# Four transformer layers on one NeuronCore: layer-norm sums taken from the additions and ScalarE, narrow products after the first wide one

## The reference, cut to what matters

```python
def layer_norm(x, g, b):
    mu = jnp.mean(xf, axis=-1, keepdims=True)
    var = jnp.mean(jnp.square(xf - mu), axis=-1, keepdims=True)
    return (xf - mu) * lax.rsqrt(var + LN_EPS) * g + b

# layers 0 and 1 (first_block)
mix = hybrid_mixer(x, w_in[l], ...)    # h @ w_in, split in nine parts: latent attention and
                                       # sparse top-64 attention, @ w_o
x = layer_norm(ALPHA * x + mix, ln1_g[l], ln1_b[l])
ffn = grouped_moe(x, ...)              # 16 experts, 2 for each token
x = layer_norm(ALPHA * x + ffn, ln2_g[l], ln2_b[l])

# layer 2: hgrn2_mixer (recurrent), layer 3: swa_sink_mixer (sliding window), each then
h = layer_norm_2(ALPHA_2 * h + mix, ln_mix_g[layer], ln_mix_b[layer])
ff = conv_ffn(h, ...)                  # 1024 -> 5632, convolution of width 3, gate, -> 1024
h = layer_norm_2(ALPHA_2 * h + ff, ln_ffn_g[layer], ln_ffn_b[layer])
# after layer 2, from its output: keys and values that layer 3 uses
k_flat, v_flat = jnp.split(h @ shared_w_kv, 2, axis=-1)
```

## Time and profile before

| | before |
|---|---|
| runs, us | 1381.19, 1379.75, 1381.02 (median 1381.02) |
| profiled execution, us | 1381.08 |
| its span, us | 1379.3 |
| mean granted TensorE clock (1 is full speed) | 0.981 |
| TensorE busy | 1309.4 us (95%) |
| weight loads on TensorE | 975.9 us (71%) |
| VectorE busy | 776.9 us (56%) |
| ScalarE busy | 563.9 us (41%) |
| GpSimd busy | 109.4 us (8%) |
| transfers | 347.64 MB, mean 252 GB/s |
| instructions | 20,721 |

### The profile page before, as it was taken

The page is one execution under the profiler, slowest core; times in us unless marked ns, Lnnn a source line. Parts: engine busy times, 40 slices in busy tenths (PEclk is TensorE's granted clock), DMA queues, the critical chain, the costliest instruction groups (busy, mean ns, idle before and its releaser), DMA issues.

```text
span 1379.3 us, 20721 instructions
## 1 busy us (share of the span) xinstructions
PE 1309.4 (95%) x8104; PEld 975.9 (71%) x8104; DVE 776.9 (56%) x1462; ACT 563.9 (41%) x1012; POOL 109.4 (8%) x130
## 2 busy tenths in 40 slices
PE   7989999999899999999989999999999988999997
PEld 7867444444686764344339988899998876999985
DVE  3976312112578651112145799877775676577766
ACT  4563211211446431111124335276654473466552
POOL 1030000000001200000002362000000011000000
PEclk9999999999999989999998999999999999999999
DMA  9338899999744579999997437685756520656630
GB/s 304 134 149 331 352 421 421 421 421 421 244 151 183 217 289 423 421 421 421 421 384 233 147 102 116 153 272 183 243 213 209 182 70 1 214 183 198 245 136 31
DMA packets 130072, 347.64 MB, mean 252 GB/s; under 512 B 10277, under 2 KB 86331, under 8 KB 105412
## 3 DMA queue, kind: packets, MB, share of 16 engines
q1 hardware_dynamic: 125232, 332.29, 63.9%
q0 software_dynamic: 3888, 13.55, 4.3%
q10 hardware_dynamic: 868, 0.63, 0.1%
HBM read 342.25 MB, written 4.19 MB: 251 GB/s over the span
## 4 chain that ended last, share of the span: by engine, by line
PE 70%; DVE 14%; DMA 7%; SPq 4%; ACT 2%; issue 2%; POOL 0%; DVEq 0%; ACTq 0%
PE bank L2032 12%; PE bank L1857 9%; PE bank L1858 8%; PE bank L1859 8%; PE bank L2043 6%; SPq L664 4%; DMA slot<-in_w_up 4%; PE bank L2366 3%; PE bank L2370 3%; PE bank L2368 3%; DMA slot<-in_ffn_w_in 2%; PE bank L1742 2%; PE bank L1808 2%; PE bank L1869 1%; DVE ln_stats L1190 1%
## 5 line engine op out<-in xcount | busy, mean ns | idle before, releaser
L1857 PE MATMUL bank<-x_high,w_high 128*128 128x256 f32 x1040 | 295.7, 284 | 0.0
L1858 PE MATMUL bank<-x_low,w_high 128*128 128x256 f32 x1040 | 294.4, 283 | 0.0
L1859 PE MATMUL bank<-x_high,w_low 128*128 128x256 f32 x1040 | 294.3, 283 | 0.0
L793 ACT ACTIVATE w_high<-slot 128x1024 fp32r<-128x1024 f32 x214 | 215.6, 1054 | 178.5 <-PE bank L1859 78.9
L2032 PE MATMUL bank<-slot,arena 128*64 128x512 f32 x976 | 223.0, 592 | 1.6 <-DMA slot<-in_w_up 1.6
L1857 PEld LDWEIGHTS bank<-x_high,w_high 128*128 128x128 f32 x1040 | 199.7, 192 | 1.8 <-issue 1.7
L1858 PEld LDWEIGHTS bank<-x_low,w_high 128*128 128x128 f32 x1040 | 199.8, 192 | 0.1
L1859 PEld LDWEIGHTS bank<-x_high,w_low 128*128 128x128 f32 x1040 | 199.7, 192 | 0.0
L2032 PEld LDWEIGHTS bank<-slot,arena 128*64 128x64 f32 x976 | 73.3, 137 | 142.5 <-issue 142.3
L1635 DVE TENSOR_TENSOR w_low<-slot,w_high 128x1024 fp32r<-128x1024 f32 x88 | 104.0, 1222 | 58.2 <-ACT w_high L793 58.2
L1456 DVE TENSOR_TENSOR arena<-arena,bank 128x512 f32<-128x512 f32 x16 | 11.0, 688 | 200.9 <-PE bank L2032 200.9
(11 more groups left out here) (345 smaller groups left out, 2196.9 us busy)
## 6 DMA issues: line engine op xcount, KB each, us to landing
slot<-in_w_gate SPq DMA_DIRECT2D x62, 1024.0 KB, 19.6
slot<-in_w_up SPq DMA_DIRECT2D x60, 1024.0 KB, 19.0
slot<-in_w_down SPq DMA_DIRECT2D x60, 1024.0 KB, 18.7
slot<-in_ffn_w_in SPq DMA_DIRECT2D x44, 1024.0 KB, 7.5
slot<-in_ffn_w_out SPq DMA_DIRECT2D x22, 1024.0 KB, 5.0
slot<-in_hgrn_w_in SPq DMA_DIRECT2D x16, 1024.0 KB, 6.7
slot<-in_w_in SPq DMA_DIRECT2D x10, 1024.0 KB, 9.8
slot<-in_w_o SPq DMA_DIRECT2D x8, 1024.0 KB, 4.9
```

Source lines behind the costliest of these rows:

```text
L793: return nc.scalar.activation(dst, src, ACT.Copy)
L1857: mm(dst, high[:, k, :], x_high[:, k, :], start=(k == 0), stop=False)
L1858: mm(dst, high[:, k, :], x_low[:, k, :], start=False, stop=False)
L1859: last = mm(dst, low[:, k, :], x_high[:, k, :], start=False, stop=(k == KD - 1))
```

## The change

**Norm.** The statistics and the aggregate go. The residual addition of each half also writes its row sum (`accum_out`) to `ln_sum`; after the experts it is the last addition of the pairs that does so. One 128x1 operation makes minus the mean from the two sums. ScalarE squares `res` with minus the mean as bias over 1024 columns and sums the squares (`accum_out`), and takes the root of that over 1024. VectorE centres with minus the mean into `x_tok` instead of `res`. In the norms behind the mixers and for the `z` norm, the order of ScalarE's roots and copies of tile 0 and 1 changes, and where `xT` is wanted in tile 1, it is copied after `x_high`.

**Waits.** The first wide product behind a norm waits for `x_high` by half: its steps 0 to 3 need only the first half of tile 1, its steps 4 to 7 the second. VectorE's `x_low` of tile 1 waits for the `xT` copies too.

**Order and banks.** `narrow(l, 1)` and `values(1)` come behind the first half of the first wide product, between its "hw" and its "x" pass. The narrow product gets a bank of its own, `ki`, where it shared `ikdk` with a wide one.

```diff
-        for n, by in (("f2", "ikdk"), ("f1", 1), ("c", 2), ("iq", 4), ("a", 6), ("b", 8), ("d", 10),
+        for n, by in (("f2", "ki"), ("f1", 1), ("c", 2), ("iq", 4), ("a", 6), ("b", 8), ("d", 10),
...
                 act.wait_ge(sem("ln_moments"), 2 * k + t + 1)
-                nc.scalar.activation(ln_std[:, t:t + 1], ln_mv[:, t, 1:2], ACT.Sqrt, bias=eps[:, 0:1]).then_inc(sem("ln_root"), 1)
+                link(nc.scalar.activation(arena[:, D * t:D * (t + 1)], res[:, t, :], ACT.Square, bias=ln_minus_mean[:, t:t + 1],
+                                          accum_out=ln_squares[:, t:t + 1]))
+                nc.scalar.activation(ln_std[:, t:t + 1], ln_squares[:, t:t + 1], ACT.Sqrt, bias=eps[:, 0:1], scale=1.0 / D).then_inc(sem("ln_root"), 1)
...
+                late = y == "z"
+                if k is not None:
+                    for t in range(1 if late else NT):
+                        std_of(k, t)
                 for t in range(NT):
-                    if k is not None and (t == 0 or not whole):
-                        std_of(k, t)
-                    if whole:
+                    if whole and t == 0:
                         copies(t, xT, "x_whole")
-                    if k is not None and whole and t == 0:
-                        std_of(k, 1)
+                        if late:
+                            std_of(k, 1)
                     copies(t, x_high, "x_high_ready")
+                    if whole and t:
+                        copies(t, xT, "x_whole")
...
+                b = produced(act, (l, "ki"))
+                drained(copy(A["ikdk"][0:N_KI, 0, :], b[0:N_KI, 0:T]), (l, "ki"))
                 b = produced(act, (l, "ikdk"))
-                copy(A["ikdk"][0:N_KI, 0, :], b[0:N_KI, 0:T])
-                drained(copy(A["ikdk"][:, 1, :], b[:, T:2 * T]), (l, "ikdk"))
+                drained(copy(A["ikdk"][:, 1, :], b[:, 0:T]), (l, "ikdk"))
...
-                            ins = V.scalar_tensor_tensor(res[:, t, cols], x_tok[:, t, cols], ALPHA, b[:, :], ALU.mult, ALU.add)
+                            ins = V.scalar_tensor_tensor(res[:, t, cols], x_tok[:, t, cols], ALPHA, b[:, :], ALU.mult, ALU.add, accum_out=ln_sum[:, t, h:h + 1])
                             drained(ins, (l, f"{y}{t}{h}"))
+                    if from_psum:
+                        for h in range(2):
                             evacuated(dve, (l, f"{y}{t}{h}"))
-                        last = V.bn_stats(ln_stats[:, t, h, :], res[:, t, cols])
-                    link(last)
-                    V.bn_aggr(ln_mv[:, t, :], ln_stats[:, t, :, :].rearrange("p a b -> p (a b)")).then_inc(sem("ln_moments"), 1)
+                    for n in (t,) if from_psum else range(NT if t == 0 else 0):
+                        V.tensor_scalar(ln_minus_mean[:, n:n + 1], ln_sum[:, n, 0:1], ln_sum[:, n, 1:2], -1.0 / D, ALU.add, ALU.mult)\
+                            .then_inc(sem("ln_moments"), 1)
                     dve.wait_ge(sem("ln_moments"), 2 * k + t + 1)
                     if k in (1, 3):
                         dve.wait_ge(sem("ln2_rows"), 32 * (k // 2 + 1))
                     else:
                         dve.wait_ge(sem("ln_rows"), 32 * ([0, 2, 4, 5, 6, 7].index(k) + 1))
-                    link(V.scalar_tensor_tensor(res[:, t, :], res[:, t, :], ln_mv[:, t, 0:1], ln_gb[:, 0, :], ALU.subtract, ALU.mult))
+                    link(V.scalar_tensor_tensor(x_tok[:, t, :], res[:, t, :], ln_minus_mean[:, t:t + 1], ln_gb[:, 0, :], ALU.add, ALU.mult))
                     dve.wait_ge(sem("ln_root"), 2 * k + t + 1)
                     link(V.reciprocal(ln_std[:, t:t + 1], ln_std[:, t:t + 1]))
                     for h, ready in enumerate(("ln_half", "ln_done")):
                         cols = slice(512 * h, 512 * (h + 1))
-                        V.scalar_tensor_tensor(x_tok[:, t, cols], res[:, t, cols], ln_std[:, t:t + 1], ln_gb[:, 1, cols], ALU.mult, ALU.add)\
+                        V.scalar_tensor_tensor(x_tok[:, t, cols], x_tok[:, t, cols], ln_std[:, t:t + 1], ln_gb[:, 1, cols], ALU.mult, ALU.add)\
                             .then_inc(sem(ready), 1)
...
+                    if t and whole_before is not None:
+                        dve.wait_ge(sem("x_whole"), 4 * whole_before + n + 1)
...
+                            if p < PAIRS - 1:
+                                drained(V.tensor_tensor(r, r, b[:, :], ALU.add), (l, f"M{t}{h}{p}"))
+                            else:
+                                drained(V.scalar_tensor_tensor(r, r, 1.0, b[:, :], ALU.mult, ALU.add, accum_out=ln_sum[:, t, h:h + 1]), (l, f"M{t}{h}{p}"))
...
-            def passes(dst, n, ab, kinds, t=None, first=False, last=False):
-
-                x = slice(0, T) if t is None else tok(t)
-                d = dst[:, T * ab:T * (ab + 1)] if t is None else dst[:, T * ab + P * t:T * ab + P * (t + 1)]
+            def passes(d, n, ab, kinds, first=False, last=False, new_x=None):
+
                 for k in range(KD):
+                    if new_x is not None and k % 4 == 0:
+                        pe.wait_ge(sem("x_high_ready"), new_x + 3 + k // 4)
                     for kind in kinds:
                         weight = (w_low if kind == "w" else w_high)[n % 2][:, ab, k, :]
-                        ins = mm(d, weight, (x_low if kind == "x" else x_high)[:, k, x], start=(first and k == 0 and kind == "h"),
+                        ins = mm(d, weight, (x_low if kind == "x" else x_high)[:, k, :], start=(first and k == 0 and kind == "h"),
...
+            def first_pair(name, n, new_x, tokens, i=None, between=None):
+
+                b = reuse(pe, name, i)
+                for ab in range(2):
+                    d = b[:, T * ab:T * (ab + 1)]
+                    pe.wait_ge(sem("split"), 2 * n + ab + 1)
+                    passes(d, n, ab, "hw", first=True, new_x=new_x)
+                    if ab == 0:
+                        if between is not None:
+                            between()
+                        transposes_out(*tokens)
+                    last = passes(d, n, ab, "x", last=True)
+                done(last, name)
...
+                return product(b[0:N_KI, tok(t)], lambda c: s2[:, c, :], lambda c: xT[:, c, tok(t)], KD)
...
-                b = narrow(l, 1)
+                b = reuse(pe, (l, "ikdk"))
                 pe.wait_ge(sem("split"), 2 * IN_UNIT[l] + 1)
-                pe.wait_ge(sem("x_high_ready"), 4 * (l + 1))
-                for k in range(KD):
-                    mm(b[:, T:2 * T], w_high[0][:, 0, k, :], x_high[:, k, :], start=(k == 0), stop=False)
-                    mm(b[:, T:2 * T], w_low[0][:, 0, k, :], x_high[:, k, :], start=False, stop=False)
+                passes(b[:, 0:T], IN_UNIT[l], 0, "hw", first=True, new_x=4 * l)
+                done(narrow(l, 1), (l, "ki"))
                 transposes_out(*((l - 1, "m") if l else (0, "in")))
-                for k in range(KD):
-                    last = mm(b[:, T:2 * T], w_high[0][:, 0, k, :], x_low[:, k, :], start=False, stop=(k == KD - 1))
-                done(last, (l, "ikdk"))
+                done(passes(b[:, 0:T], IN_UNIT[l], 0, "x", last=True), (l, "ikdk"))
...
-                b = reuse(pe, (l, "U00"), 0)
-                pe.wait_ge(sem("x_high_ready"), before_x + 4)
-                for ab in range(2):
-                    pe.wait_ge(sem("split"), 2 * n + ab + 1)
-                    passes(b, n, ab, "hw", first=True)
-                    if ab == 0:
-                        transposes_out(l, y)
-                    last = passes(b, n, ab, "x", last=True)
-                done(last, (l, "U00"))
+                first_pair((l, "U00"), n, before_x, (l, y), 0)
...
-            done(values(1), (3, "vv"))
-            transposes_out(2, "z")
-            pair(3, "kv0", KV_UNIT)
+            first_pair((3, "kv0"), KV_UNIT, 16, (2, "z"), between=lambda: done(values(1), (3, "vv")))
```

34 lines of the change are left out of this document (19 added, 15 removed).

## The result

The changed kernel took 1383.73 us in the median of 16 runs (1381.40 to 1385.59), the kernel before 1379.74 in as many on the same chip: a ratio of 1.0033, 95% interval 1.0023 to 1.0043. So it is 4.0 us slower, clear of the 0.2% bound; the forecast was 4.2 us slower.

What follows compares the result with a forecast made beforehand. The chain that ended last ran through TensorE for 70% of the span, VectorE second with 14%. Losses of 7.15 less gains of 2.92 made it 4.2 us slower than 1381.1: 1385.3 us, range 1381.2 to 1388.5.

Steps and rivals of the forecast that it cites:

- Wait ahead of kv0, 3.2 us: Before kv0: its first pass waits for the weight split, no longer covered by values(1); loss 3.2 us.
- Clock behind it, 1.7 us: Behind kv0's start: 3.9 us of TensorE idle time is followed by half clock; loss 1.7 us (0 to 3.4).
- the clock holds: Rival: no half clock behind kv0, everything else as forecast without the 1.7; 1383.6 us, chance 0.22.
- both idle times: Rival: idle time at layer 0's start drops the clock as at kv0, 1.7 us more; 1387.0 us, chance 0.20.
- Start of layer 0, 1.9 us: Start of layer 0: the second narrow product comes behind a split product whose start does not move; loss 1.9 us.
- Norm prices: Norms: mean to x_tok 3.20 us in tile 0 with the table load, 1.90 without; closing norm gains 0.24.
- No drain: Rival on ScalarE's table switches: a second 1.28 us each makes tile 0 late for TensorE; 1391 us, chance 0.03.
- Mixer norms, loss 0.35 in layer 0 and 0 in layer 1: First two mixer norms: ScalarE's tile-1 copies come later, loss 0.35 us in layer 0, 0 in layer 1.
- Layer 1's experts, gain 1.1: MoE norm of layer 1: earlier x_tok and a product needing fewer x_high copies; gain 1.1 us (0.3 to 1.3).
- Layer 0's experts, gain 0.45: MoE norm of layer 0: half-block product needs only the first x_high copy; gain 0.45 us (0 to 0.6).
- After the recurrent mixer, gain 0.93: Norm after the recurrent mixer: tile 1's transposes move forward, capped by filler; gain 0.93 us (0.5 to 0.93).
- The 72-column products have a bank of their own now ... 0: Narrow products' own bank: one more ScalarE copy empties it, TensorE meets the wait only later; cost 0.

Runs made afterwards that it cites:

- experiment 1: Changed kernel with both narrow products ahead again and tile 1's xT copied before x_high; 1375.62 us, ratio to before 0.9968.
- experiment 3: Changed kernel with eight filler products on TensorE in the idle time ahead of kv0; 1381.68 us, ratio to before 1.0014.
- experiment 4: Kernel before with values(1) placed behind the first pass of kv0, nothing else changed; 1385.37 us, ratio to before 1.0044.
- experiment 5: Changed kernel with narrow products ahead again and a dummy root ahead of each norm's first square; 1375.85 us, ratio to before 0.9971.
- experiment 7: Changed kernel with only narrow(l, 1) ahead of the first wide product again at the starts of layers 0 and 1; 1382.30 us, ratio to before 1.0017.
- experiment 2: Changed kernel with a one-column dummy root ahead of each norm's first square, to load the table early; 1380.19 us, ratio to before 1.0002.
- experiment 10: Kernel before with one edit: the first wide product behind a norm waits for x_high by half; 1378.24 us, ratio to before 0.9978.
- experiment 8: Kernel of experiment 1, but TensorE waits for all of x_high before the first wide product; 1380.95 us, ratio to before 1.0007.
- experiment 11: Changed kernel with the old turn of PSUM banks from layer 1's last norm on; 1381.97 us, ratio to before 1.0014.
- experiment 12: Changed kernel with narrow products ahead, dummy root, 2 instead of 8 fillers behind the experts, old bank turn in layers 2 and 3; 1374.39 us, ratio 0.9961.

## Why the prediction was right, point by point

- **Wait ahead of kv0, 3.2 us:** right. Product start moved by no more than the split allows, values(1) behind it; 54.95-50.22 = 4.73 us in all, 3.2 without the clock (experiments 1, 3, 4).
- **Clock behind it, 1.7 us:** right, 1.55. The rival "the clock holds" fell.
- **Clock at the start:** none in the profile of the changed kernel. In experiment 3's the same stretch took 41.93 instead of 40.41 at a clock of 0.56 in 15 to 18 us, so the rival "both idle times" is true of some runs. But slow products stand there with the old order too: in experiment 5 the 32 narrow records took 5.77 us instead of 3.93, and the stretch 40.12. That the idle time is the cause isn't shown here.
- **Start of layer 0, 1.9 us:** right, 40.41-38.67 = 1.74; experiment 7 takes it away.
- **Norm prices:** 3.20 and 1.90 us forecast, 3.19 and 1.91 measured. The sum beside an addition is not quite free: 0.08 us each, and the mean's operation 0.21 instead of 0.17. So tile 0 was 0.99 later, tile 1 1.00 earlier, and the closing norm's gain 0 instead of 0.24.
- **No drain:** the root follows the load after 0.02 us in the path itself. By the Trainium skill (ScalarE: Activation LUTs, "What ACT_TABLE_LOAD costs") it would have been 2.66 us for the switch; 1.28 was measured, and the measurement decides. The prediction calls the change the opposite of the advice to group calls by table set. That was a wrong reading: ScalarE loads a table 37 times before, after and in experiment 2, so the change and the preload only move loads.
- **Mixer norms, loss 0.35 in layer 0 and 0 in layer 1:** too small. The router's product waits 0.65 us in each, 1.3 in all. From tile 1's transposes to the first expert product it takes 15.7 to 15.8 us in the new-norm traces of layer 0 and 15.1 before (traces with a long half-clock stretch apart). For layer 1 "those copies waited longer for TensorE" was read off a profile with half clock just there: experiment 4, at full clock, has the same 0.17 us of slack as layer 0.
- **Layer 1's experts, gain 1.1:** 1.27 at the product's start (0.8 to 2.3 in the new-norm traces with eight fillers and waits by half). Waits by half carry 0.8 of it (experiment 10), the norm by itself none (8).
- **Layer 0's experts, gain 0.45:** wrong. The transposes came 0.6 us later, by the fillers' wait for a bank. The gain by the order is there, but smaller: from tile 1's transposes to the x pass 5.20 us instead of 5.50.
- **After the recurrent mixer, gain 0.93:** by VectorE's first addition it looks true (1.00), on TensorE it isn't. From tile 0's transposes to the product it takes 7.04 us before and 7.90 and 7.55 in the two other old-norm kernels (4, 10), and 6.98 to 7.91 in the nine traces with new norms and turned banks: no gain that can be told from chance. With the banks turned back it is 5.62 (11, 12), so norm and waits win something there, and the turned bank takes 1.4 of it back. The cap by the fillers holds: in those two traces tile 1's transposes follow them without a wait.
- **After the sliding-window mixer, gain 0.2:** from tile 1's addition to the product 6.04 instead of 6.07: 0, again the bank (5.42 in experiment 11).
- **The step that failed** is "The 72-column products have a bank of their own now ... 0". I priced the new job where it is used, not what it does to the round of banks behind it. It cost 0.6 us in layer 0, 1.4 in layer 2 and 0.6 behind layer 3's mixer, and it saved 1.0 or more ahead of layer 3's output projection.
- **Not forecast:** the end. 0.9 us more from x_tok's last write to the end of the span, below.

Losses by the traces: kv0 4.7 (wait and clock), start 1.7, the two mixer norms 1.3, layer 0's experts 0.3, the end 0.9, together 8.9. Gains: layer 1's experts 1.3, layer 3 from its attention to the transposes 2.1, together 3.4. That makes 5.5; by runs it is 4.0. The rest is open; each profile has its own half-clock stretches: from a product in layer 1's mixer to one in its expert stage old-norm kernels took 122.14, 119.02 and 122.16 us (before, 4 and 10). That the forecast is within 0.2 us is therefore partly luck: kv0 and the start, most of the losses, were right to a few tenths. The mixer norms, layer 0's experts, the gains behind the two later mixers and the end came out some 4 us worse than forecast, and layer 3's bank and the clock set most of that off.

## What to carry over

A product that needs nothing late belongs ahead of one that waits, not behind it: price a reorder by what TensorE has to do while the split is made. When a planner hands out banks in turn, adding one job moves every job behind it; list who used each bank last, before and after, for the better as well as for the worse. Measure a stage between marks on the engine that carries the chain: by VectorE's first addition a gain of 1.0 us stood where TensorE had none. And compare kernels by the stretch and by the mean clock of their runs: single profiles of one kernel differ here by more than the change is worth.

## What the runs showed of the hardware

- The mean granted clock of a run goes with most of the scatter (two thirds of the variance within a kernel): 0.72 us for each 0.001. Experiment 8's runs went from 1375.98 to 1384.84 us.
- In the nine traces with the turned banks the span ends 4.0 us after the last write of x_tok, in the five others (before, 4, 10, 11, 12) 3.1. Of the two output transfers of 512 KB the first lands 2.7 us after its issue in all; the second 2.7 in the five and 3.6 in the nine. Neither what follows it in the queues nor the norms explain it: experiment 11 has the new norms and 3.1. The cause is open.
- The idle time of 3.96 us ahead of kv0 was followed by a granted clock of 0.50 and 0.71; with filler products in it the clock stayed at 1.00 (experiment 3).
- A sum beside an operation (`accum_out`) shows as an instruction of its own: 0.08 us on VectorE, 0.18 on ScalarE.
